# A transformer kernel on one core: the load, turning and rounding of the input at its start are rearranged

## The chip, the cores and the metric

The kernel runs on one core of a Trainium2 chip. The metric is the device time of one execution in microseconds, the median of several runs. One core has five engines that run their own instruction lists: TensorE (PE: matmuls; its weight loads are listed as PEld), VectorE (DVE), ScalarE (ACT), GpSimd (POOL) and SyncE (SP), which here only issues DMAs. They wait for one another through semaphores, and each one works strictly in the order of its list.

## The reference

Two blocks of a transformer over 256 positions of width 1024: the first has two layers, and each begins with a gated feed-forward part. What the change touches is only the very beginning, the first feed-forward part of the first layer:

```python
def rms_norm(x, g):
    y = xf * lax.rsqrt(jnp.mean(xf * xf, axis=-1, keepdims=True) + EPS)
    return (y * g)

def swiglu(x, w_gate, w_up, w_down):
    return (jax.nn.silu(x @ w_gate) * (x @ w_up)) @ w_down

h = x
h = h + 0.5 * swiglu(rms_norm(h, ffn1_norm_g[0]), ffn1_w_gate[0], ffn1_w_up[0], ffn1_w_down[0])
hn = rms_norm(h, mix_norm_g[0])
# mixing, a second feed-forward part; then the second layer and the second block
```

## The kernel before

**Arithmetic.** Everything is float32. A product of float32 matrices is made of three products of rounded halves: x = x_hi + x_lo and w = w_hi + w_lo, where the high half is the value rounded to the type that TensorE multiplies in one pass (fp32r), and the low half is the rounded rest; w_lo by x_lo is left out. The activations are kept turned (channels in partitions, 256 positions along the free axis), in eight chunks c of 128 channels; `hT` is the residual stream, `x_hi` and `x_lo` (`xh`, `xl`) are its halves multiplied by the gain `gcol` of the norm. The factor of the norm per position is applied later, to the product.

**Slots.** All weights pass through 403 slots of 128x1024 float32 (512 KB), in an order written out by `weight_plan`. SP loads slot j into one of seven raw buffers (it waits until `lo` of slot j-7 is made). ACT rounds it (`whi`, L1295, signal `hi`), DVE subtracts (`wlo`, L1896, signal `lo`), and TensorE consumes it in order. The split of slot j (`split_to`) also waits until TensorE has used slot j-5. When ACT and DVE come to `use(slot)`, they split up to slot+4.

**The matmuls of a slot** (`part`, `block`, L504): eight blocks, each a matmul of w_hi by both halves of x (512 columns) and one of w_lo by x_hi (256 columns). The first block of a slot waits for `hi` before its first and for `lo` before its second matmul. Slots 0 to 3 are the first pair of the first feed-forward part: slot 0 is gate, chunks 0 to 3; slot 1 up, chunks 0 to 3; slot 2 gate, chunks 4 to 7; slot 3 up, chunks 4 to 7. In slots 0 and 2 each chunk also waits for its `x_hi` and `x_lo`. Before slot 3 stand the sums of squares for the norm (`norm_sums`, four matmuls of `ones`, which wait for the last `square_sums`, that is `acc(0,3)`). Slot 4 begins when DVE has added the two halves of slot 2's product (`sum` of gate 0; ACT copies one half first, L1342, DVE adds, L1970).

**The start.** SP issues the gain row, the two tiles of 128 positions of `x` (512 KB each), then slots 0 to 3, then seven more gain rows, then the slots from 4 on. TensorE turns the gain row (8 transposes, L688), then `x`: 16 transposes (L696) into banks 0 to 3, one bank for each pair p of chunks, with a signal `x{p}` after each. ACT copies pairs 1 and 3 to `hT`, DVE pairs 0 and 2. Then ACT makes x_hi from `hT` (L1372, two for each pair), and after pairs 0 and 1 the w_hi of slots 0 and 1; DVE makes x_lo (L1988) and w_lo likewise. Then ACT squares the four pairs (L1362, the fourth waits for the first sum) and DVE adds them up (L1982, three times, `acc`). Slots 2 to 4 are split after that, by `use(0)`. On GpSimd masks and constants are made until 16.7 us (`ident` first, `alib` from 3.35 to 14.4 us).

Of the kernel before, what the change touches and what calls it, by code (L numbers as in the profile page):

```python
# [328 lines left out]
def signals(nc, ctx):  # L329
# [28 lines left out]
    s.ld_x = [sig(f"ld_x{i}", ["all"], 16) for i in T2]  # L358
# [56 lines left out]
    s.h_act = sig("h_act", [1, 3])  # L415
# [38 lines left out]
    s.h = sig("h", [(0, 0), (0, 2)] + [(v, p) for v in range(1, 7) for p in P4])  # L454
# [43 lines left out]
def tensor_engine(nc, B, s):  # L498
# [185 lines left out]
    def start():  # L684
        pe.wait_ge(*s.consts.at("ident"))
        pe.wait_ge(*s.ld_g0.at("all"))
        for c in range(8):
            t = pe.transpose(bank[4][:, c:c + 1], B.grow[0:1, c * 128:(c + 1) * 128], ident[0:1, 0:1])  # L688
        t.then_inc(*s.pe_set.now("g0"))
        for p in range(4):  # L690
            for tt in range(2):
                if p == 0:
                    pe.wait_ge(*s.ld_x[tt].at("all"))
                for j in range(2):
                    c = 2 * p + j
                    t = pe.transpose(bank[p][:, j * 256 + tt * 128:j * 256 + (tt + 1) * 128],  # L696
                                     B.xn[:, tt, c * 128:(c + 1) * 128], ident[:])
            t.then_inc(*s.pe_set.now(f"x{p}"))


    def ffn(f, x, gen):
        base, F = FFN[f], B.ffn[f]
        for p in range(PAIRS):
# [10 lines left out]
            if p:  # L714
                cols(x, 8, up_slot(f, p), 0)
                pe.wait_ge(*s.sum.at(("up", f, p - 1)))
                cols(x, 8, up_slot(f, p) + 2, 2)
            else:
                part(x, base, 0, range(4), True, False, gen)
                if f in (1, 3):  # L720
                    pe.wait_ge(*s.h.at((2, 2) if f == 1 else (5, 1)))
                elif f == 2:
                    pe.wait_ge(*s.sum.at(("up", 1, PAIRS - 1)))
                part(x, base + 1, 2, range(4), True, False)
                part(x, base + 2, 0, range(4, 8), False, True, gen)
# [554 lines left out]
def scalar_engine(nc, B, A, s):  # L1280
# [1558 lines left out]
def sync_engine(nc, B, A, s):  # L2839
# [99 lines left out]
```

## Time and profile before

| | us |
|---|---|
| median of 3 runs | 1253.1 |
| the runs | 1253.06, 1253.10, 1255.51 |
| the profiled execution, its own time | 1250.83 |
| its span in the trace | 1249.6 |
| TensorE busy | 1220.2 |

The span is the stretch of the trace from the first to the last instruction; 1.2 us of the execution's own time lie around it. A timeline row gives the start, the duration and the instruction; several of a kind in succession are merged into one row with their count (x14). In brackets is how long the engine stood idle before it and who released it. "L504" is the line of the helper in which all the products are written, so the names of the tiles tell which product it is: out<-in.

### The profile page before, as it was taken

The numbers are of one execution on the slowest core, as the hardware profiler recorded it, in microseconds if no ns is written. First come the engines' busy times: TensorE is split into PE (matmuls) and PEld (weight loads), VectorE is DVE, ScalarE is ACT, GpSimd is POOL, SyncE is SP. The second block draws the span as 40 slices with busy tenths as digits, with TensorE's granted clock in tenths as the row PEclk, the third lists the DMA queues.
The fourth block names the chain that finished last, engine by engine and source line by source line (L and its number), as shares of the span: only waits on it lengthen the run. The fifth ranks groups of instructions, "written<-read, shape, count | busy, mean of one in ns | idle before, by whom it ended". The sixth has DMA issues, their size and how long they took to land.

```text
span 1249.6 us, 18894 instructions
## 1 busy us (share of the span) xinstructions
PE 1220.2 (98%) x7518; PEld 1069.8 (86%) x7518; DVE 881.7 (71%) x1255; ACT 682.0 (55%) x1033; POOL 60.7 (5%) x89
## 2 busy tenths in 40 slices
PE   7999999989999999999999999999999999899998
PEld 6888888867888888888888887988888899788996
DVE  6686856885787766777766667587776668565875
ACT  5655544533665555555654457556655445555463
POOL 4000100100010000000000122000000000000000
PEclk9999999999999999999999999999999999999999
DMA  8766566771566655666655555156665665646450
GB/s 273 233 206 188 165 189 192 205 183 42 164 195 184 195 172 177 194 192 189 192 183 163 176 190 165 35 152 197 191 194 177 184 188 169 174 118 156 144 174 34
DMA packets 205653, 215.46 MB, mean 172 GB/s; under 512 B 9808, under 2 KB 192592, under 8 KB 205566
## 3 DMA queue, kind: packets, MB, share of 16 engines
q1 hardware_dynamic: 202998, 210.76, 56.8%
q10 hardware_dynamic: 2568, 3.50, 0.9%
q8 instruction: 60, 0.98, 0.3%
q14 instruction: 27, 0.22, 0.0%
HBM read 212.19 MB, written 2.03 MB: 171 GB/s over the span
## 4 chain that ended last, share of the span: by engine, by line
PE 92%; ACT 3%; DVE 2%; issue 1%; DMA 0%; ACTq 0%; POOL 0%; SPq 0%
PE psum L504 90%; ACT whi L1295 1%; DVE wlo L1896 1%; PE psum L668 0%; DMA xn<-in_x 0%; PE psum L953 0%; ACT qn L1599 0%; PE psum L696 0%; ACT L1735 0%; ACTq L1410 0%; DVE small L2333 0%; DVE oa L2543 0%; PE psum L1108 0%; ACT qkc L1699 0%; PE psum L906 0%
## 5 line engine op out<-in xcount | busy, mean ns | idle before, releaser
L504 PE MATMUL psum<-x,whi 128*128 128x512 f32 (+1 forms) x2288 | 696.2, 365 | 5.3 <-ACT whi L1295 2.4
L1896 DVE TENSOR_TENSOR wlo<-raw,whi 128x1024 fp32r<-128x1024 f32 (+2 forms) x403 | 474.3, 1189 | 193.3 <-ACT whi L1295 190.0
L504 PE MATMUL psum<-x,wlo 128*128 128x256 f32 x1960 | 549.3, 280 | 0.8 <-DVE wlo L1896 0.8
L1295 ACT CAST whi<-raw 128x1024 fp32r<-128x1024 f32 (+2 forms) x403 | 406.2, 1022 | 171.6 <-PE psum L504 162.5
L504 PEld LDWEIGHTS psum<-x,whi 128*128 128x128 f32 x2288 | 409.4, 189 | 79.6 <-ACT whi L1295 2.8
L504 PEld LDWEIGHTS psum<-x,wlo 128*128 128x128 f32 x1960 | 371.3, 189 | 1.5 <-DVE wlo L1896 1.3
L504 PE MATMUL psum<-g,whi 128*128 128x512 f32 x704 | 247.7, 396 | 0.0
L504 PE MATMUL psum<-g,wlo 128*128 128x256 f32 x704 | 197.6, 281 | 0.0
L504 PEld LDWEIGHTS psum<-g,whi 128*128 128x128 f32 x704 | 132.3, 188 | 31.8
L504 PE MATMUL psum<-whi,x 128*128 128x512 f32 (+1 forms) x512 | 141.2, 376 | 4.7 <-ACT va L1768 3.3
L504 PEld LDWEIGHTS psum<-g,wlo 128*128 128x128 f32 x704 | 132.2, 188 | 0.0
L504 PEld LDWEIGHTS psum<-whi,x 128*128 128x128 f32 x512 | 90.2, 190 | 21.1 <-ACT va L1768 3.5
L504 PE MATMUL psum<-wlo,x 128*128 128x512 f32 (+1 forms) x256 | 86.6, 374 | 0.0
L1342 ACT COPY pr<-psum 128x512 f32<-128x512 f32 x44 | 25.8, 586 | 66.9 <-PE psum L504 66.9
L1342 ACT COPY gr<-psum 128x512 f32<-128x512 f32 x44 | 25.8, 586 | 61.1 <-PE psum L504 61.1
L1970 DVE TENSOR_TENSOR pr<-psum,pr 128x512 f32<-128x512 f32 x44 | 30.4, 690 | 35.5 <-ACT pr L1342 35.5
L504 PEld LDWEIGHTS psum<-wlo,x 128*128 128x128 f32 x256 | 46.1, 189 | 8.6
L1372 ACT ACTIVATE x<-hT,gcol 128x256 fp32r<-128x256 f32 x64 | 28.5, 500 | 45.3 <-DVE hT L2105 28.8
L1970 DVE TENSOR_TENSOR gr<-psum,gr 128x512 f32<-128x512 f32 x44 | 30.4, 690 | 31.1 <-ACT gr L1342 31.0
L1988 DVE SCALAR_TENSOR_TENSOR x<-hT,gcol,x 128x256 fp32r<-128x256 f32 x64 | 28.7, 495 | 18.2 <-ACT x L1372 18.2
L1431 ACT ACTIVATE gr<-gr 128x512 f32<-128x512 f32 x44 | 27.6, 632 | 21.4 <-DVE gr L2054 21.3
L1440 ACT CAST g<-pr 128x512 fp32r<-128x512 f32 x44 | 27.4, 622 | 19.3 <-DVE pr L2062 19.3
(321 smaller groups left out, 851.1 us busy)
## 6 DMA issues: line engine op xcount, KB each, us to landing
raw<-in_ffn_w_gate SPq DMA_DIRECT2D x88, 512.0 KB, 4.5
raw<-in_ffn_w_up SPq DMA_DIRECT2D x88, 512.0 KB, 4.2
raw<-in_ffn_w_down SPq DMA_DIRECT2D x80, 512.0 KB, 3.8
raw<-in_w_in SPq DMA_DIRECT2D x52, 512.0 KB, 3.8
raw<-in_w_o SPq DMA_DIRECT2D x16, 512.0 KB, 4.7
raw<-in_a_w_in SPq DMA_DIRECT2D x14, 512.0 KB, 4.7
raw<-in_w_kv SPq DMA_DIRECT2D x16, 384.0 KB, 3.3
raw<-in_w_mem_kv SPq DMA_DIRECT2D x8, 512.0 KB, 3.7
```

What stands on the lines that cost most here:

```text
L504: return pe.matmul(o, l, r, start=start, stop=stop, skip_group_check=True)
L1295: act.copy(held(B.whi[:, i % SPLIT, :], *n), held(B.raw[:, i % RAW, :], *n)).then_inc(*s.hi.now(i))
L1342: act.copy(out, psum[:, b:b + 2, S:2 * S]).then_inc(*s.half.now(key))
L1372: act.activation(x[:, c, :], hT[:, c, :], ACT.Copy, scale=gcol[:, c, gi:gi + 1]).then_inc(*s.x_hi.now((gen, c)))
L1431: act.activation(r, r, ACT.Silu).then_inc(*s.silu.now((f, p)))
L1440: act.copy(F.gh[:, 2 * p:2 * p + 2, :], in_pairs(F.pr[:, p % 2, :])).then_inc(*s.g_hi.now((f, p)))
L1896: dve.tensor_tensor(held(B.wlo[:, i % SPLIT, :], *n), held(B.raw[:, i % RAW, :], *n), held(B.whi[:, i % SPLIT, :], *n).bitcast(F32), ALU.s ...
L1970: dve.tensor_tensor(out, psum[:, b:b + 2, 0:S], out, ALU.add).then_inc(*s.sum.now(key))
L1988: dve.scalar_tensor_tensor(out=xl[x][:, c, :], in0=hT[:, c, :], scalar=gcol[:, c, gi:gi + 1], in1=xh[x][:, c, :].bitcast(F32), op0=ALU.mul ...
```

## The change

- **Load.** The left 512 columns of `x` are loaded first (two DMAs of 256 KB), then slots 0 and 1, then the right 512 columns, then slots 2 and 3 and the rest as before. The first gain row is issued by ACT instead of SP.
- **TensorE.** After the gain row it does ten float32 matmuls of `ident` by `ident` (128x128, results not used), turns chunks 0 to 3 of `x` into banks 4 and 5, does six more such matmuls, and begins slot 0. The other eight transposes, into banks 6 and 7, stand in the middle of slot 1, after its fourth block.
- **ACT** makes x_hi straight from PSUM as each pair is turned, and splits one slot after each pair: slots 0 to 3. It copies no `hT`. Each of its squares waits for its pair of `hT`.
- **DVE** makes x_lo straight from PSUM and w_lo of the same slot, pair by pair; after pairs 1 and 3 it copies two pairs of `hT` (four copies in all, two before). The sums of squares stand behind all of this.

```diff
@@ TensorE, start
+            t = pe.transpose(bank[3][:, c:c + 1], B.grow[0:1, c * 128:(c + 1) * 128], ident[0:1, 0:1])
         t.then_inc(*s.pe_set.now("g0"))
+        warm(10)
+        x_turn("left", (0, 1))
+        warm(6)
+
+    def warm(n):
+        for _ in range(n):
+            mm(bank[2][:, 0:128], ident[:], ident[:], True, True)
+
+    def x_turn(side, pairs):
+        for tt in range(2):
+            pe.wait_ge(*s.ld_x[side, tt].at("all"))
+            for p in pairs:
                 for j in range(2):
                     c = 2 * p + j
-                    t = pe.transpose(bank[p][:, j * 256 + tt * 128:j * 256 + (tt + 1) * 128],
+                    t = pe.transpose(bank[4 + p][:, j * 256 + tt * 128:j * 256 + (tt + 1) * 128],
                                      B.xn[:, tt, c * 128:(c + 1) * 128], ident[:])
-            t.then_inc(*s.pe_set.now(f"x{p}"))
+                if tt == 1:
+                    t.then_inc(*s.pe_set.now(f"x{p}"))
@@ TensorE, ffn, slot 1
-                part(x, base + 1, 2, range(4), True, False)
+                part(x, base + 1, 2, range(4), True, False, None, (lambda: x_turn("right", (2, 3))) if f == 0 else None)
@@ ScalarE, squares and start
         if p == 0:
+            act.wait_ge(*s.h.at((v, 0)))
...
+            if v == 0:
+                act.wait_ge(*s.h.at((v, p)))
...
-        for p in (1, 3):
-            act.wait_ge(*s.pe_set.at(f"x{p}"))
-            act.copy(flat(hT[:, 2 * p:2 * p + 2, :]), bank[p]).then_inc(*s.h_act.now(p))
+        act.dma_start(B.grow[0:1, :], A["ffn1_norm_g"][0:1]).then_inc(*s.ld_g0.now("all"))
         act.wait_ge(*s.gcol.at("g0"))
         for p in range(4):
-            if p % 2 == 0:
-                act.wait_ge(*s.h.at((0, p)))
-            elif p == 1:
-                act.wait_ge(*s.h_act.at(3))
-            prep(0, p, [("f0", 0, xh[0])])
-            if p < 2:
-                split_to(p)
+            act.wait_ge(*s.pe_set.at(f"x{p}"))
+            for c in (2 * p, 2 * p + 1):
+                act.activation(xh[0][:, c, :], bank[4 + p][:, (c % 2) * S:(c % 2 + 1) * S], ACT.Copy,
+                               scale=gcol[:, c, 0:1]).then_inc(*s.x_hi.now(("f0", c)))
+            split_to(p)
@@ VectorE, start
-        for p in (0, 2):
-            dve.wait_ge(*s.pe_set.at(f"x{p}"))
-            dve.tensor_copy(flat(hT[:, 2 * p:2 * p + 2, :]), bank[p]).then_inc(*s.h.now((0, p)))
         for p in range(4):
-            prep(0, p, [("f0", 0, 0)])
-            if p < 2:
-                split_to(p)
+            dve.wait_ge(*s.x_hi.at(("f0", 2 * p + 1)))
+            for c in (2 * p, 2 * p + 1):
+                dve.scalar_tensor_tensor(out=xl[0][:, c, :], in0=bank[4 + p][:, (c % 2) * S:(c % 2 + 1) * S],
+                                         scalar=gcol[:, c, 0:1], in1=xh[0][:, c, :].bitcast(F32), op0=ALU.mult,
+                                         op1=ALU.subtract).then_inc(*s.x_lo.now(("f0", c)))
+            split_to(p)
+            if p % 2:
+                for q in (p - 1, p):
+                    dve.tensor_copy(flat(hT[:, 2 * q:2 * q + 2, :]), bank[4 + q]).then_inc(*s.h.now((0, q)))
@@ SyncE
-    sp.dma_start(B.grow[0:1, :], gains[0]).then_inc(*s.ld_g0.now("all"))
-    for tt in range(2):
-        sp.dma_start(B.xn[:, tt, :], A["x"][0, tt * 128:(tt + 1) * 128, :]).then_inc(*s.ld_x[tt].now("all"))
+    def x_load(side, c0):
+        for tt in range(2):
+            sp.dma_start(B.xn[:, tt, c0:c0 + 512], A["x"][0, tt * 128:(tt + 1) * 128, c0:c0 + 512]).then_inc(
+                *s.ld_x[side, tt].now("all"))
+
+    x_load("left", 0)
     for j, (w, k0, nk, c0, n) in enumerate(weight_plan(A)):
+        if j == 2:
+            x_load("right", 512)
```

## Rows read from the trace of the kernel before

**Rows 1.** The page: the chain that ended last, share of the span by engine.

```profile
PE 92%; ACT 3%; DVE 2%; issue 1%; DMA 0%; ACTq 0%; POOL 0%; SPq 0%
```

**Rows 2.** Waits of PE, whole span (columns: us in total, times, longest).

```profile
PE psum L504 <- issue: 5.9, 3, 4.4
PE psum L504 <- ACT va L1768: 3.3, 1, 3.3
PE psum L504 <- ACT whi L1295: 2.4, 1, 2.4
PE psum L696 <- DMA xn<-in_x: 2.3, 2, 1.6
```

**Rows 3.** Timeline of 0 to 10 us: start, duration, instruction, idle time before it.

```profile
0.79 0.34 SPq L2865 DMA_DIRECT2D gnm<-in_ffn_norm_g  x1
...
1.18 0.84 SPq L2867 DMA_DIRECT2D xn<-in_x  x2
...
2.28 0.98 PE L688 MATMUL psum<-ident,gnm 1*128 1x1 f32 x8 [2.28 <-DMA gnm<-in_ffn_norm_g]
...
4.90 0.69 PE L696 MATMUL psum<-ident,xn 128*128 128x128 f32 x2 [1.64 <-DMA xn<-in_x]
...
6.29 3.25 PE L696 MATMUL psum<-ident,xn 128*128 128x128 f32 x14 [0.71 <-DMA xn<-in_x]
...
7.02 0.69 DVE L2033 COPY hT<-psum 128x512 f32<-128x512 f32 x1 [3.55 <-PE psum L696]
```

**Rows 4.** Timeline of 10 to 14 us, all engines.

```profile
10.06 0.91 ACT L1372 ACTIVATE x<-hT,gcol 128x256 fp32r<-128x256 f32 x2
...
10.87 1.03 ACT L1295 CAST whi<-raw 128x1024 fp32r<-128x1024 f32 x1
...
11.94 1.55 DVE L1896 TENSOR_TENSOR wlo<-raw,whi 128x1024 fp32r<-128x1024 f32 x1 [0.45 <-ACT whi L1295]
...
12.56 1.86 POOL L2750 TENSOR_SCALAR_AFFINE_SELECT alib<-alib 128x1024 bf16<-128x1024 bf16 x1
...
13.41 1.70 DVE L1988 SCALAR_TENSOR_TENSOR x<-hT,gcol,x 128x256 fp32r<-128x256 f32 x2
...
13.54 0.58 PE L504 MATMUL psum<-x,wlo 128*128 128x256 f32 x1 [0.79 <-DVE wlo L1896]
```

**Rows 5.** Timeline of PE around 18 us: two block starts.

```profile
17.76 0.63 PE L504 MATMUL psum<-x,whi 128*128 128x512 f32 x1
...
18.39 0.40 PE L504 MATMUL psum<-x,whi 128*128 128x512 f32 x1
```

**Rows 6.** Timeline of DVE and ACT, 16 to 26 us.

```profile
16.19 1.66 DVE L1988 SCALAR_TENSOR_TENSOR x<-hT,gcol,x 128x256 fp32r<-128x256 f32 x4
17.78 2.27 DVE L1982 TENSOR_TENSOR acc<-acc,sqb 128x512 f32<-128x512 f32 x3
20.09 5.77 DVE L1896 TENSOR_TENSOR wlo<-raw,whi 128x1024 fp32r<-128x1024 f32 x5
...
19.03 4.84 ACT L1295 CAST whi<-raw 128x1024 fp32r<-128x1024 f32 x5
```

**Rows 7.** Timeline of PE at the square sums and the starts of slots 3, 4.

```profile
24.07 0.95 PE L504 MATMUL psum<-ones,acc 128*128 128x4 f32 x8
24.88 0.48 PE L504 MATMUL psum<-x,whi 128*128 128x512 f32 x1
...
27.74 0.39 PE L504 MATMUL psum<-x,whi 128*128 128x512 f32 x1
```

**Rows 8.** Timeline of PE: the norm rows of slot 5.

```profile
30.52 0.60 PE L504 MATMUL psum<-diag,ones 128*128 128x128 f32 x4
```

**Rows 9.** Windows after PE's longest gap; PEclk stands after the busy times.

```profile
272.00:274.00 2.00, 2.00 (x24) 1.34 (x20) 1.28 (x3) 0.00 (x0) 0.00 (x0) 0.50 1.10 348
274.00:276.00 2.00, 2.00 (x36) 1.14 (x27) 0.00 (x0) 0.00 (x0) 0.00 (x0) 0.91 0.54 182
```

**Rows 10.** DMA issues of 2.0 to 2.4 us: size each, us to landing.

```profile
raw<-in_ffn_w_gate SPq DMA_DIRECT2D x1, 512.0 KB, 5.7
```

More of the change, by code:

```diff
@@ L357, in signals @@
     s.ld_g0 = sig("ld_g0", ["all"], 16)
-    s.ld_x = [sig(f"ld_x{i}", ["all"], 16) for i in T2]
+    s.ld_x = {(d, i): sig(f"ld_x_{d}{i}", ["all"], 16) for d in ("left", "right") for i in T2}
     s.ld_gr = sig("ld_gains", range(1, 8), 16)
@@ L414, in signals @@
     s.row = sig("norm_row", NORM_ROWS)
-    s.h_act = sig("h_act", [1, 3])
     s.sq = sig("squares", h_pairs)
@@ L453, in signals @@
     s.gcol = sig("gain_cols", ["g0", "all"])
-    s.h = sig("h", [(0, 0), (0, 2)] + [(v, p) for v in range(1, 7) for p in P4])
+    s.h = sig("h", h_pairs)
     s.acc = sig("square_sums", [(v, p) for v in range(7) for p in range(1, 4)])
@@ L687, in start @@
         for c in range(8):
-            t = pe.transpose(bank[4][:, c:c + 1], B.grow[0:1, c * 128:(c + 1) * 128], ident[0:1, 0:1])
+            t = pe.transpose(bank[3][:, c:c + 1], B.grow[0:1, c * 128:(c + 1) * 128], ident[0:1, 0:1])
         t.then_inc(*s.pe_set.now("g0"))
-        for p in range(4):
-            for tt in range(2):
-                if p == 0:
-                    pe.wait_ge(*s.ld_x[tt].at("all"))
+        warm(10)
[8 more added lines that the diff above has]
+            for p in pairs:
                 for j in range(2):
                     c = 2 * p + j
-                    t = pe.transpose(bank[p][:, j * 256 + tt * 128:j * 256 + (tt + 1) * 128],
+                    t = pe.transpose(bank[4 + p][:, j * 256 + tt * 128:j * 256 + (tt + 1) * 128],
                                      B.xn[:, tt, c * 128:(c + 1) * 128], ident[:])
-            t.then_inc(*s.pe_set.now(f"x{p}"))
+                if tt == 1:
+                    t.then_inc(*s.pe_set.now(f"x{p}"))
     def ffn(f, x, gen):
@@ L2029, in start @@
         dve.wait_ge(*s.pe_set.at("g0"))
-        dve.tensor_copy(gcol[:, :, 0], bank[4][:, 0:8]).then_inc(*s.gcol.now("g0"))
-        for p in (0, 2):
-            dve.wait_ge(*s.pe_set.at(f"x{p}"))
-            dve.tensor_copy(flat(hT[:, 2 * p:2 * p + 2, :]), bank[p]).then_inc(*s.h.now((0, p)))
+        dve.tensor_copy(gcol[:, :, 0], bank[3][:, 0:8]).then_inc(*s.gcol.now("g0"))
         for p in range(4):
-            prep(0, p, [("f0", 0, 0)])
-            if p < 2:
-                split_to(p)
+            dve.wait_ge(*s.x_hi.at(("f0", 2 * p + 1)))
[7 more added lines that the diff above has]
+                    dve.tensor_copy(flat(hT[:, 2 * q:2 * q + 2, :]), bank[4 + q]).then_inc(*s.h.now((0, q)))
         for p in range(4):
@@ L2864, in sync_engine @@
              A["ffn2_norm_g"][1:2], A["norm_pre_2"][0:1]]
-    sp.dma_start(B.grow[0:1, :], gains[0]).then_inc(*s.ld_g0.now("all"))
-    for tt in range(2):
-        sp.dma_start(B.xn[:, tt, :], A["x"][0, tt * 128:(tt + 1) * 128, :]).then_inc(*s.ld_x[tt].now("all"))
+    def x_load(side, c0):
[3 more added lines that the diff above has]
+    x_load("left", 0)
     for j, (w, k0, nk, c0, n) in enumerate(weight_plan(A)):
+        if j == 2:
+            x_load("right", 512)
         if j == 4:
```

1 line of the change is left out of this document (removed).

## The prediction

> **What bounds the kernel now.** I read the chain that ended last first: 92% of it is TensorE, next to nothing is DMA [rows 1]. Then the list of what TensorE waited for [rows 2]. Its waits are few, each behind another engine that works on a product of TensorE's own. Only at the start does it wait for data. From slot 4 on nothing is tied to the clock on the wall, so whatever the start wins or loses should reach the end one to one. I therefore follow the start to one mark, the first matmul of slot 4, at 27.74 us [rows 7], and compare times there.
>
> The path to that mark now: the input lands, TensorE turns it from 4.90 to 9.54 us [rows 3]; ACT rounds x from 10.06 and slot 0 from 10.87, DVE makes its rest from 11.94 to 13.49, and at 13.54 TensorE goes on [rows 4]. From there it never stops. A block starts 0.63 us after the one before it at 17.76 [rows 5], but a whole slot of eight takes 27.74 - 24.88 = 2.86 us later, 0.357 a block [rows 7]: TensorE ran at 1.2 GHz until about 18.2 us and at 2.4 GHz after it. The granted clock shows the lower level only where it fell within the span: 0.50 in 272 to 274 us and 0.91 in 274 to 276 [rows 9], after the wait of 4.4 us; the wait of 3.3 us is not followed by such a stretch [rows 2]. DVE has done the last sum of squares at 20.05 [rows 6], and TensorE asks for it at 24.07 [rows 7]: 4 us to spare.
>
> **Load and constants.** The gain row stays first on its queue, now ACT's, with nothing ahead of it; I take the same arrival and the same end of its transposes, 3.26 us [rows 3]. If ACT's queue were slower, all shifts by that. SP comes to x 0.4 us sooner, with half the bytes ahead of slot 0, which now lands at about 2.1 + 5.7 = 7.8 us [rows 10]; the left half is there by 4.9 at the latest. Neither is late for what follows, because ten matmuls of constants stand ahead of the transposes. The trace has no such matmul by name, but its like: the norm rows are two float32 matmuls in the code and four records in the trace [rows 8], the sums of squares four and eight [rows 7]. So ten constants are twenty passes. One pass at 1.2 GHz I take from the transposes of the same shape: 14 in 3.25 and 2 in 0.69 [rows 3] make 2.56 / 12 = 0.213 us. At 2.4 GHz it is half, 0.107. Bounds: 10 x 0.107 = 1.1 us (one pass each, full clock) and 20 x 0.232 = 4.6. I take 20 x 0.213 = 4.3, end at 7.55.
>
> When does the clock rise? In this trace TensorE had worked for 4.65 us from 13.54, and from 270.64 (after the long wait) until about 274.4, 3.7 us. Counted from the gain row or from the first constant that is 5.9 to 7.9; I take 7.5. Then six transposes at 0.107 and the 0.27 until the last is through put pair 0 at 8.4. The price of the bounds: a rise at 5.9 saves 1.6 / 0.213 x 0.107 = 0.8 us, one at 9.2 or later costs six transposes at 0.107, 0.65, and some blocks, in all 1.0.
> The Trainium skill (TensorE: Matmul & The Clock Gate, What's actually happening) says that the number of slow matmuls at the start varies between runs of one kernel, and not to fit a model to one count; by that the 7.5 is not a property of the kernel, and the sum would be anything between the two bounds. The single trace here cannot show that spread.
>
> **To slot 0.** Pair 0 is there at 8.4; ACT needs 0.91 for x_hi and 1.03 for the rounding [rows 4], 10.4; DVE 1.23 for w_lo (five in 5.77 are 1.15 each and a tail, [rows 6]): 11.7 against 13.49. Gain 1.8 us: the copy to `hT` is off this path. The six later constants take 0.64 to 1.3 us and lie in TensorE's wait for ACT: nothing. x_hi straight from PSUM is not in the trace; a DVE operation of 512 columns from PSUM takes 0.69 [rows 3], about two rests of 256 (0.83, [rows 6]), so I take the same cost, with 0.1 us either way for each of four steps on the path, 0.4.
> DVE was slow while GpSimd ran its select on `alib` (12.56 to 14.42): 1.55 for a w_lo that takes 1.23 elsewhere, 1.70 for two x_lo where four take 1.66 [rows 4, 6]. Two x_lo of pair 1 will again fall at 11.7; at the slow rate w_lo of slot 1 comes at 14.9, 0.4 late.
> The Trainium skill (GPSIMD Engine Reference, Key points) says that GpSimd and VectorE contend where a VectorE instruction has two inputs in SBUF; an x_lo from PSUM has one, so by the rule it would keep its 0.42 us each and the 0.4 would be gone. I leave them out of the sum and in the range.
>
> **Slot 0.** If the clock has risen before it, 0.357 a block: from the arrival of w_lo 2.86 - 0.24 = 2.6 us instead of 18.39 - 13.54 = 4.85 [rows 4, 5]. Gain 2.25; end at 14.3. TensorE then idles at most some 1.3 us ahead of it, and even 3.3 us cost no clock [rows 2].
>
> **Slot 1** now holds eight transposes: 8 x 0.107 = 0.87 lost (they stood ahead of everything before). End at 14.3 + 2.86 + 0.87 = 18.0.
>
> **Slot 2 is where a new wait comes.** ACT and DVE can do nothing for it until pair 2 is turned: 14.3 + 4 x 0.357 + 5 x 0.107 + 0.27 = 16.55. Then x_hi 0.91 and the rounding of slot 2, 1.03, queued behind it: 18.5; w_lo 1.23: 19.8. TensorE would have been through slot 2 at 20.9; it now gets there at 19.8 + 2.6 = 22.4. Loss 1.5.
>
> **Slot 3 is where the second comes,** the sums of squares. DVE's list after w_lo of slot 2: two x_lo 0.83, w_lo of slot 3 1.15, two copies of `hT` 1.3 (0.69 each, overlapping), then the three sums with ACT's square between them, which took 20.09 - 17.78 = 2.3 [rows 6]. That is 19.8 + 5.6 = 25.4; TensorE asks at 22.4. Loss 3.0; the 4 us to spare are gone, because `hT` of the right half is copied only behind slot 3's split. Sums and slot 3 take 0.81 + 2.86 [rows 7], end at 29.05.
>
> **Slot 4.** Slots 4 to 6, which DVE split at 20 to 26 us beside TensorE [rows 6], now queue behind the sums: from 25.7 (ACT rounds slot 4 after its last square) 3 x 1.15, to 29.2, then the sum of gate 0, 0.69: 29.85. Loss 0.8. Mark: 29.85 against 27.74.
>
> **Sum.** -1.8 - 2.25 + 0.87 + 1.5 + 3.0 + 0.8 = 2.1 us later. The profiled execution, 1250.8, would be 1252.9. It lies 2.3 below the median of the runs shown; the shift is added to the median: 1253.1 + 2.1 = 1255.2. Own range of this case: 0.8 + 0.4 down and 1.0 + 0.4 + 0.4 up, 1254.0 to 1257.0. What a measurement of this kernel can tell from no change is about 0.2%, 2.5 us, so most of this case counts as the same.
>
> **Rivals.**
> - **The clock stays low (slower).** The change doesn't do what it says: matmuls of constants, or what the later gaps leave of them, don't lift the clock, as 3.25 us of transposes up to 9.54 did not [rows 3]. It decides if the rise comes after slot 0. Then pair 0 is ready at 9.1, 0.7 later, and slots 0 and 1 run some 9 to 14 blocks at 0.63 instead of 0.357, 2.5 to 3.8 us: 2.1 + 0.7 + 3.2 = 6.0 less some of the waits behind, about 5.3: 1258.4. For it: the same rows; against it: the stretch now is 6 us long and unbroken.
> - **The constants are short.** One pass each, 2.1 us, end at 5.4, pair 0 at about 6.9 with the clock up in the meantime: 1.5 less, +0.6, 1253.7. Against it: the doubled records [rows 7, 8].
> - **The waits at slots 2 to 4 don't come (faster).** If ACT and DVE had slack for the right half, by much cheaper operations from PSUM, 5.3 us of loss would vanish and 3.2 of gain stay: 1249.9. It takes halving DVE's 5.6 us behind slot 2 and more, and its nearest rows (0.69 from PSUM, 1.15, 2.3) give nothing of the kind. Halfway there the result is the same as before.
>
> **How the numbers follow.** The forecast gets 0.62, the low clock 0.12, short constants 0.16, no waits 0.10. Slower by over 2.5 us: the low clock, and of the forecast, with an error of a run's median of a microsecond, 0.36 of it: 0.12 + 0.22 = 0.34. Faster: 0.10 and little of the short constants: 0.12. Same: 0.54. The range leaves out the last rival and the upper half of the low clock: 1251.3 to 1258.3.
>
> **What would show it.** Twenty records of constants from 3.3 to about 7.6 us; pair 0 turned at 8.4; blocks 0.36 apart from the first of slot 0; TensorE idle for about 1 us before the second matmul of slot 2, about 3 us before the matmuls of `ones` and `acc`, under 1 us before slot 4, the releasers w_lo, the last `acc` and the gate sum on DVE; from there on the same waits as before. The prediction is wrong if a block of slot 0 takes 0.63, if the sums of squares come before TensorE asks, or if the gain row comes later on ACT's queue.

## The result, and the profile after

| | before | after |
|---|---|---|
| median, us | 1253.1 | 1259.5 |
| the runs, us | 1250.4 to 1255.5 | 1258.0 to 1260.3 |
| the profiled execution, us | 1250.8 | 1259.8 |
| its span, us | 1249.6 | 1258.6 |
| first product of slot 4, us | 27.74 | 32.57 |

The ratio of after to before is 1.0044, with a 95% interval of 1.0032 to 1.0057: 4.0 to 7.1 us slower, 5.5 in the middle. Forecast were 2.1 slower and a range that ended at 1258.3. The direction is right, the size forecast was under half of what came.

The chain that ended last is TensorE's as before (page of after, shares of the span; it answers to [rows 1]), so the difference lies in what TensorE waited for:

```profile
PE 91%; ACT 3%; DVE 3%; issue 1%; ACTq 0%; DMA 0%; POOL 0%
```

Waits of TensorE in after (us in total, times, longest), which answer to [rows 2]. The first is new; those for w_lo and w_hi are now two each:

```profile
PE psum L503 <- DVE acc L1990: 2.5, 1, 2.5
PE psum L503 <- DVE wlo L1904: 2.4, 2, 1.7
...
PE psum L503 <- ACT whi L1305: 1.9, 2, 1.6
```

Timeline of after, 0 to 14 us, all engines (the product's helper is L503 here); it answers to [rows 3, 4]:

```profile
3.18 4.29 PE L503 MATMUL psum<-ident 128*128 128x128 f32 x20
...
7.30 1.04 PE L705 MATMUL psum<-ident,xn 128*128 128x128 f32 x8
...
8.18 1.50 PE L503 MATMUL psum<-ident 128*128 128x128 f32 x12
8.21 1.28 ACT L1409 ACT_TABLE_LOAD   x1 [8.21 <-PE psum L705]
...
11.29 1.07 POOL L2759 TENSOR_SCALAR_AFFINE_SELECT alib<-alib 128x1024 bf16<-128x1024 bf16 x1
11.31 2.13 DVE L1904 TENSOR_TENSOR wlo<-raw,whi 128x1024 fp32r<-128x1024 f32 x1
...
11.33 0.50 PE L503 MATMUL psum<-x,whi 128*128 128x512 f32 x1 [1.65 <-ACT whi L1305]
...
12.50 1.85 POOL L2761 TENSOR_SCALAR_AFFINE_SELECT alib<-alib 128x1024 bf16<-128x1024 bf16 x1
13.36 0.86 DVE L2042 SCALAR_TENSOR_TENSOR x<-psum,gcol,x 128x256 fp32r<-128x256 f32 x2
...
13.49 0.39 PE L503 MATMUL psum<-x,wlo 128*128 128x256 f32 x1 [1.66 <-DVE wlo L1904]
```

These two rows stand in the timeline of the kernel before, 0 to 14 us:

```profile
0.79 1.28 ACT L1394 ACT_TABLE_LOAD   x1 [0.79 <-PEq L2929]
...
11.32 1.09 POOL L2748 TENSOR_SCALAR_AFFINE_SELECT alib<-alib 128x1024 bf16<-128x1024 bf16 x1
```

The ten constants are twenty records and end when they should. But at 8.21 us, when pair 0 is there, ACT first loads its activation table for 1.28 us; before, the same load stood at 0.79 us and cost nothing. And DVE's first w_lo takes 2.13 us beside GpSimd's selects, so TensorE goes on at 13.49, where it had gone on at 13.54.

That the two times are so near is no accident. In both kernels w_lo ends 1.08 us after the end of GpSimd's first select (12.36 and 13.44 in after, 12.41 and 13.49 before), though it began at 11.31 in one and at 11.94 in the other. So w_hi, ready 0.6 us earlier in after, gained nothing: DVE got no further until the select was over.

Then the clock. Windows of after (busy us of PE, PEld, DVE, ACT, POOL, then PEclk, DMA share, GB/s):

```profile
14.00:16.00 2.00, 2.00 (x8) 1.64 (x7) 2.00 (x4) 0.00 (x0) 1.57 (x4) 0.50 1.09 346
16.00:18.00 2.00, 2.00 (x10) 1.73 (x9) 0.63 (x2) 0.00 (x0) 0.42 (x2) 0.70 1.09 348
```

TensorE had worked without a pause until 9.7 us and was at 2.4 GHz (twelve passes in 1.50 us, 8.18 to 9.68). It then waited 1.65 us, did one matmul, waited 1.66 us, and from about 13.9 to 17.2 us the granted clock was 0.50. Slot 0 ran at 0.64 us a block again.

The second half of the start, which answers to [rows 6, 7]:

```profile
21.80 0.49 PE L503 MATMUL psum<-x,whi 128*128 128x512 f32 x1 [0.25 <-ACT whi L1305]
...
23.06 0.39 PE L503 MATMUL psum<-x,wlo 128*128 128x256 f32 x1 [0.77 <-DVE wlo L1904]
...
26.04 2.28 DVE L1990 TENSOR_TENSOR acc<-acc,sqb 128x512 f32<-128x512 f32 x3
...
28.41 3.50 DVE L1904 TENSOR_TENSOR wlo<-raw,whi 128x1024 fp32r<-128x1024 f32 x3
...
28.47 1.03 PE L503 MATMUL psum<-ones,acc 128*128 128x4 f32 x8 [2.55 <-DVE acc L1990]
...
32.57 0.50 PE L503 MATMUL psum<-x,whi 128*128 128x512 f32 x1 [0.19 <-DVE gr L1978]
```

Here is what the prediction's steps for slots 2 to 4 describe: the short waits of slot 2, 2.55 us for the last `acc`, then DVE's three splits and the gate sum. At slot 4 after is 4.83 us behind. By 51.93 (46.36 before) it is 5.57, 0.6 of the growth being one DMA issue on ACT's queue that took 1.04 us instead of 0.45. Up to 815 us nothing is added. That 5.57 is what the ratio gives (5.5; the two medians are 6.4 apart). The rest of the 9.0 between the two spans comes at late waits, and the run of the kernel before shows below that such losses come without the change too.

### The profile page after: what moved, and what is told of

The parts are those of the page before. It is cut to its first block, busy times and chain, and to the rows that moved or that the text cites. A ratio compares the mean times of both kernels' runs of the same rounds, so it can differ in the third digit from the quotient of the medians.

```text
span 1258.6 us, 18961 instructions
## 1 busy us (share of the span) xinstructions
PE 1227.1 (97%) x7550; PEld 1077.1 (86%) x7550; DVE 883.0 (70%) x1257; ACT 680.6 (54%) x1031; POOL 60.4 (5%) x89
## 4 chain that ended last, share of the span: by engine, by line
PE 91%; ACT 3%; DVE 3%; issue 1%; ACTq 0%; DMA 0%; POOL 0%
PE psum L503 90%; DVE wlo L1904 1%; ACT whi L1305 1%; PE psum L667 0%; PE psum L963 0%; ACT qn L1607 0%; ACT qT L1668 0%; ACTq L1418 0%; ACT L1743 0%; DVE small L2344 0%; DVE oa L2554 0%; PE psum L1118 0%; ACT qkc L1707 0%; PE psum L916 0%; PE psum L1255 0%
## 5 line engine op out<-in xcount | busy, mean ns | idle before, releaser
L503 PE MATMUL psum<-x,whi 128*128 128x512 f32 (+1 forms) x2288 | 696.8, 366 | 5.6 <-ACT zob L1716 2.0
L503 PE MATMUL psum<-x,wlo 128*128 128x256 f32 x1960 | 550.4, 281 | 2.4 <-DVE wlo L1904 2.4
L503 PEld LDWEIGHTS psum<-x,whi 128*128 128x128 f32 x2288 | 410.4, 190 | 79.2 <-ACT zob L1716 2.4
L503 PEld LDWEIGHTS psum<-x,wlo 128*128 128x128 f32 x1960 | 372.3, 190 | 3.1 <-DVE wlo L1904 3.1
L503 PE MATMUL psum<-g,whi 128*128 128x512 f32 x704 | 247.7, 396 | 0.0
L503 PE MATMUL psum<-g,wlo 128*128 128x256 f32 x704 | 197.9, 281 | 0.0
L503 PEld LDWEIGHTS psum<-g,whi 128*128 128x128 f32 x704 | 132.4, 188 | 31.7
L503 PE MATMUL psum<-whi,x 128*128 128x512 f32 (+1 forms) x512 | 143.0, 380 | 4.7 <-ACT va L1776 3.3
L503 PEld LDWEIGHTS psum<-g,wlo 128*128 128x128 f32 x704 | 132.2, 188 | 0.0
L503 PEld LDWEIGHTS psum<-whi,x 128*128 128x128 f32 x512 | 91.3, 192 | 21.2 <-ACT va L1776 3.5
L503 PE MATMUL psum<-wlo,x 128*128 128x512 f32 (+1 forms) x256 | 87.4, 377 | 0.0
L503 PEld LDWEIGHTS psum<-wlo,x 128*128 128x128 f32 x256 | 46.7, 191 | 8.9
L1384 ACT ACTIVATE x<-hT,gcol 128x256 fp32r<-128x256 f32 x56 | 25.0, 500 | 45.3 <-DVE hT L2116 28.8
L1996 DVE SCALAR_TENSOR_TENSOR x<-hT,gcol,x 128x256 fp32r<-128x256 f32 x56 | 24.4, 484 | 17.0 <-ACT x L1384 17.0
```

What stands on the lines that cost most here:

```text
L503: return pe.matmul(o, l, r, start=start, stop=stop, skip_group_check=True)
L1384: act.activation(x[:, c, :], hT[:, c, :], ACT.Copy, scale=gcol[:, c, gi:gi + 1]).then_inc(*s.x_hi.now((gen, c)))
L1996: dve.scalar_tensor_tensor(out=xl[x][:, c, :], in0=hT[:, c, :], scalar=gcol[:, c, gi:gi + 1], in1=xh[x][:, c, :].bitcast(F32), op0=ALU.mul ...
```

## The experiments

The first product of slot 4 is the mark, as in the prediction (27.74 before, 32.57 after). Medians are read with the ratio to runs of the kernel before on the same chip. Every mark is from one trace, and the two don't go together one to one: e7_onlyconst has its mark 1.5 us later and the same median as the kernel before, e12_wholerows_noconst 3.9 earlier and a median that is, by the ratio, only 0.8 to 3.4 lower.

**e4_before: the kernel before again.** No edit.

> The kernel before once more, to see its own spread and how its granted clock goes with its time. In the changed kernel's trace 3.4 of the 9.0 us come at two late waits of TensorE (3.3 us at 1093, 2.0 us at 1145), after which its matmuls ran at 1.2 GHz; in the trace of before they didn't. If that is chance from run to run, some executions of before have it too: spans from 1249 to 1254 us, the longer ones with a lower mean clock (0.992 or less against 0.996). If it belongs to the change: all executions within 1 us of one another and a clock of 0.996.

Measured: ratio 0.999 (0.9981 to 0.9999), 1250.9 to 1255.3 us, mark at 27.70. The same window at TensorE's late wait of 3.3 us, first in the first trace of the kernel before, then in this one:

```profile
1090.00:1095.00 5.00, 3.26 (x16) 2.69 (x17) 1.97 (x4) 3.30 (x8) 0.00 (x0) 1.00 0.10 40
```

```profile
1090.00:1095.00 5.00, 2.38 (x6) 1.92 (x7) 1.51 (x4) 4.16 (x9) 0.00 (x0) 0.75 0.26 95
1095.00:1100.00 5.00, 5.00 (x25) 4.17 (x24) 1.61 (x5) 1.75 (x6) 0.00 (x0) 0.91 0.37 105
```

In the same program the clock falls after this wait in one execution and not in another. In after's trace it fell there for longer (18 matmuls in 6.31 us, which took 3.69 before):

```profile
1096.84 6.31 PE psum L503 x18
```

Over 96 executions of the kernel before (all those that the experiments ran), the eight with a mean granted clock of 0.996 took 1250.8 us on average, the 36 with 0.994 took 1253.5, the eleven with 0.990 took 1255.5. So the kernel's spread of 5 us goes largely with its clock, and the late falls in after's trace need be no work of the change. Whether the change makes them more frequent was not tried. The chance half of the expectation holds; the 0.992 and 0.994 groups, hardly apart (1253.7 and 1253.5), say that the mean clock is not all of it.

**e1_table: the table load moved out of the path.**

```diff
         act.dma_start(B.grow[0:1, :], A["ffn1_norm_g"][0:1]).then_inc(*s.ld_g0.now("all"))
+        act.wait_ge(*s.consts.at("ones"))
+        act.activation(small[0:1, 319:320], B.ones[0:1, 0:1], ACT.Copy)
         act.wait_ge(*s.gcol.at("g0"))
```

> One element is copied by ACT right after the gain row's DMA, so that the activation table is loaded at about 2 us and not at 8.21 us behind the wait for pair 0. My theory, that the table load stands on the path and pushes w_lo of slot 0 into GpSimd's select: x_hi from about 8.25 us, w_lo of slot 0 takes about 1.3 us instead of 2.13 and ends at about 11.3 (13.4 in the changed kernel), slot 0 runs at 2.4 GHz, 0.36 us a block from its first, and the first matmul of slot 4 comes 3.0 to 3.8 us earlier than in the changed kernel (32.57). Median about 1256. Rival, that GpSimd's work alone slows w_lo: the start is 1.3 us earlier, but w_lo still takes about 2 us and the clock still falls: 1.3 us or less, about 1258.

Measured: ratio 1.0018 (1.0001 to 1.0035), median 1256.6; w_lo of slot 0 takes 1.23 us and ends at 11.0; slot 0 at 0.35 us a block; the mark is 29.42. ACT, then DVE:

```profile
1.33 1.28 ACT L1406 ACT_TABLE_LOAD   x1 [1.33 <-PEq L2948]
```

```profile
9.77 1.23 DVE L1906 TENSOR_TENSOR wlo<-raw,whi 128x1024 fp32r<-128x1024 f32 x1
```

Slot 3 begins 3.96 us earlier than in after (25.39 against 29.35). But then the clock fell in this trace, after the 2.59 us wait for `acc` (timeline row, then the window):

```profile
24.50 1.03 PE L503 MATMUL psum<-ones,acc 128*128 128x4 f32 x8 [2.59 <-DVE acc L1992]
```

```profile
28.00:30.00 2.00, 2.00 (x8) 1.71 (x7) 1.05 (x4) 0.34 (x1) 0.73 (x1) 0.50 1.06 360
```

What follows: the table load cost more than its 1.28 us, since it also pushed w_lo into GpSimd's select and stretched TensorE's wait. The waits behind slot 1 are untouched by it. Here w_lo of slot 1 (11.70 to 12.92) was under way before the select, and this time the select waited:

```profile
11.85 1.99 POOL L2761 TENSOR_SCALAR_AFFINE_SELECT alib<-alib 128x1024 bf16<-128x1024 bf16 x1
```

It took 1.99 us for its 1.07. The two engines seem to take turns by whole instructions; that is read from these rows and was not tried by itself.

**e6_poollater: GpSimd's selects after w_lo of slot 1.** Built on after.

```diff
+        pool.wait_ge(*s.lo.at(1))
         step(pool.affine_select(out=B.alib[:, 0], in_=B.alib[:, 0], compare_op=ALU.is_ge, ...
```

> Built on the changed kernel: GpSimd starts its two selects on alib only after DVE has made w_lo of slot 1. If the selects made w_lo of slot 0 slow: 1.23 us instead of 2.13, it ends at 12.55 instead of 13.45 and the mark comes 0.9 us earlier; the idle stretch of TensorE shrinks from 1.66 to 0.8 us before it, and if the clock then stays up, another 1.6: median 1257 to 1258.6. If something else made it slow (the DMA writes into the raw buffers, say): 2.1 us again and no change.

Measured: ratio 1.0034 (1.0021 to 1.0048), median 1257.7, 1257.5 to 1258.7. w_lo takes 1.23 us and no block of slot 0 is slow, though pair 0 was there only at 9.5, because the eight transposes still ran at 1.2 GHz (1.74 us, 1.04 in after):

```profile
12.61 1.23 DVE L1904 TENSOR_TENSOR wlo<-raw,whi 128x1024 fp32r<-128x1024 f32 x1
```

TensorE waited 1.61 and 0.76 us around its first matmul, and the clock stayed up. The mark is 31.38, 1.2 earlier than in after. It was the selects that slowed w_lo; the loads went on as before.

**e3_bridge: more constants.** The second group is 14 instead of 6.

```diff
-        warm(6)
+        warm(14)
```

> The second group of constants is 14 instead of 6, so TensorE works until about 11.2 us instead of 9.7. If the clock fell at about 13.9 because TensorE had been idle or nearly so since 9.7, it now stays up: slot 0 at 0.36 us a block, its end 1.6 us earlier, slot 4 1.6 us earlier, since the chain of DVE starts from the middle of slot 1: median about 1257.9. Rival, that this length doesn't matter, as it is the wait for w_lo that counts: the clock falls as before and nothing changes, 1259.5.

Measured: ratio 1.0035 (1.0018 to 1.0053), median 1257.8, 1254.0 to 1261.9. The constants now reach up to the first product, and the blocks after the wait are 0.35 apart:

```profile
8.62 3.29 PE L503 MATMUL psum<-ident 128*128 128x128 f32 x28
...
13.50 0.39 PE L503 MATMUL psum<-x,wlo 128*128 128x256 f32 x1 [1.23 <-DVE wlo L1904]
13.72 0.40 PE L503 MATMUL psum<-x,whi 128*128 128x512 f32 x1
...
14.07 0.40 PE L503 MATMUL psum<-x,whi 128*128 128x512 f32 x1
```

The clock stayed up through slot 0, as the theory wanted; in this trace it fell after the wait for `acc` instead (blocks 0.64 apart from 28.85 on), and the mark is 32.22, 0.35 before that of after. One fall was traded for another. The median moved by what was expected, but with a spread of 8 us that is no proof.

**e2_noconst: no constants at all.** Both `warm` calls are taken out of after.

> Both groups of constants (ten and six) are left out. If the constants cost more than they bring, because the clock falls again before slot 0 anyway: pair 0 is turned at about 5.5 us instead of 8.1, the table load and the roundings follow, w_lo of slot 0 ends at about 10.2, all of slot 0 and some of slot 1 run at 1.2 GHz (2.9 us lost for the ten blocks instead of 1.6), and slot 4 begins 1.5 to 2.5 us earlier than in the changed kernel: median about 1257.5. Rival, that the constants earn their place: the whole start at 1.2 GHz costs more than 3 us, median 1260 or more.

Measured: ratio 1.0026 (1.0016 to 1.0036), median 1257.6. The transposes begin at 3.67 and w_lo of slot 0 is there at 9.7, at 1.2 GHz:

```profile
3.67 1.97 PE L703 MATMUL psum<-ident,xn 128*128 128x128 f32 x8
...
9.68 0.58 PE L503 MATMUL psum<-x,wlo 128*128 128x256 f32 x1 [0.47 <-DVE wlo L1902]
```

Slot 0 ran at 0.64 us a block until 13.3, and the mark is 29.77, 2.8 us earlier than in after. The first ten constants held the transposes back by 3.6 us, more than the clock gave back; the theory that they cost more than they bring holds. 0.9 of the gain comes by way of GpSimd: w_lo was over (9.63) before the first select began, and took 1.23 us instead of 2.13.

**e5_asklater: the sums of squares are asked for one slot later.** Built on e1_table; the norm rows behind them move by one slot too.

```diff
-NORM = ((3, 5), (75, 4), (101, 4), (169, 4), (237, 0), (269, 6), (337, 4))
+NORM = ((4, 5), (75, 4), (101, 4), (169, 4), (237, 0), (269, 6), (337, 4))
```

> Built on e1_table: the sums of squares are asked for before slot 4 instead of before slot 3 (and the norm rows before slot 6). In e1_table TensorE waits 2.6 us there, from 21.9 to 24.5, and its clock falls afterwards. If that wait is the loss: slot 3 runs at once, slot 4 begins 2 us or more earlier than in e1_table, median about 1254. If DVE's total work is the bound, as I think: TensorE now waits before slot 4 for the gate sum, which DVE ends at about 28.5 us as before, and the sums come on top, 0.9; slot 4's first product at about 29.4, 0.7 later than in e1_table. What is won is only the clock, up to 1.5 us in those executions in which it falls: 1256 to 1257.

Measured: ratio 1.0037 (1.0022 to 1.0052), median 1258.6, so no faster than e1_table (the two intervals overlap). Slot 3 begins at once, at 22.0, and TensorE then waits 3.83 us for the gate sum:

```profile
28.82 1.87 PE L503 MATMUL psum<-ones,acc 128*128 128x4 f32 x8 [3.83 <-DVE gr L1980]
```

DVE ends that sum at 28.77, in e1_table at 28.55. So the wait for `acc` is not the loss; it is where DVE's backlog shows first. Taken away there, it comes back one slot later and longer. After it the clock fell again, and the first product of slot 4 came at 30.55, later than the 29.4 expected.

**e9_turnfirst: the right half turned ahead of slot 0.** Built on e1_table.

```diff
         x_turn("left", (0, 1))
         warm(6)
+        x_turn("right", (2, 3))
...
-                part(x, base + 1, 2, range(4), True, False, None, (lambda: x_turn("right", (2, 3))) if f == 0 else None)
+                part(x, base + 1, 2, range(4), True, False)
```

> Built on e1_table: the eight transposes of the right half stand after the second group of constants, ahead of slot 0, instead of in the middle of slot 1. Everything else, DVE's order with its late copies and sums too, stays. If the late turning is what makes the waits at slots 2 and 3: w_lo of slot 2 is made at about 16.5 us (19.1 in e1_table), no wait before slot 2, slot 2 ends at about 19.5, and the wait before slot 3 begins sooner but ends sooner too, at about 22 (24.5 in e1_table). Slot 4 at about 26 instead of 28.9 to 30: median about 1253.5. If DVE's work alone sets the end of slot 3's wait: it still ends at 24 or later, 1256.

Measured: ratio 1.0001 (0.999 to 1.0012), median 1254.4. Mark 26.49:

```profile
22.40 1.03 PE L503 MATMUL psum<-ones,acc 128*128 128x4 f32 x8 [2.18 <-DVE acc L1993]
...
26.49 0.50 PE L503 MATMUL psum<-x,whi 128*128 128x512 f32 x1 [0.18 <-DVE gr L1981]
```

DVE works from 9.52 to 26.4 with no gap of more than 0.1 us. In e1_table it stood idle for 2.77 us ahead of its x_lo at 16.89, until pair 2 had come through TensorE and ACT:

```profile
16.89 0.88 DVE L2044 SCALAR_TENSOR_TENSOR x<-psum,gcol,x 128x256 fp32r<-128x256 f32 x2 [2.77 <-ACT x L1411]
```

DVE's list begins 0.69 us later than in e1_table (9.52 against 8.83) and saves the 2.77 of that gap: 2.08 net, and its gate sum indeed ends at 26.44 instead of 28.55, 2.11 earlier. The rest of what the mark gained on the 29.42 of e1_table is that trace's fallen clock. So the late turning is the cause of the waits at slot 2, which are gone, and it put DVE's gate sum, and slot 4 with it, 2.1 us later. The wait for `acc` is hardly shorter (2.18 us, 2.59 in e1_table); it only lies earlier: there DVE's order, with its late copies and sums, is the likely cause, since e8_whole and e11_wholerows, whose order differs (and not it alone), have no such wait. With the late turning and the table load gone, the change costs nothing that the ratio shows, and with constants and all it gains nothing either.

**e7_onlyconst: constants alone in the kernel before.**

```diff
         t.then_inc(*s.pe_set.now("g0"))
+        warm(3)
         for p in range(4):
...
             t.then_inc(*s.pe_set.now(f"x{p}"))
+        warm(8)
```

> The kernel before with constants alone: three after the gain row and eight after the last transpose of x, both inside waits of TensorE (1.6 and 2.4 us). If constants raise the clock and cost nothing inside a wait: the transposes begin at 4.9 as before, slot 0's w_lo comes at 13.5 as before, and slot 0 runs at 0.36 us a block instead of 0.64: slot 1 starts 2.2 us earlier, the mark 2 us earlier if DVE keeps up (it has 4 us to spare at the sums, but slots 2 to 6 queue behind them), median 1251.5 to 1252. Rival: DVE has no such slack, its split of slot 2 (from 20.1 us) and of the slots behind is the next bound, then at most 1 us is won, 1253.

Measured: ratio 0.9998 (0.9988 to 1.0008), median 1253.5. Slot 0 and slot 1 ran at 0.35 us a block, as hoped, and ended at 18.9. Then slot 2 wasn't there, because ACT splits slots 2 to 6 only behind its squares. ACT, then TensorE:

```profile
18.98 4.82 ACT L1300 CAST whi<-raw 128x1024 fp32r<-128x1024 f32 x5
```

```profile
20.06 0.49 PE L504 MATMUL psum<-x,whi 128*128 128x512 f32 x1 [0.82 <-ACT whi L1300]
21.32 0.39 PE L504 MATMUL psum<-x,wlo 128*128 128x256 f32 x1 [0.76 <-DVE wlo L1901]
```

```profile
22.00:24.00 2.00, 2.00 (x8) 1.71 (x8) 2.00 (x3) 1.80 (x2) 0.00 (x0) 0.50 0.66 193
```

Waits of 0.82 and 0.76 us, and at about 22 us the clock fell; the mark is 29.20, 1.5 later than without constants. The rival holds: 2.2 us won in slots 0 and 1 were given back, in this trace and more; the ratio says neither gain nor loss.

**e10_halfloads: the kernel before with four loads of half rows.**

```diff
-    for tt in range(2):
-        sp.dma_start(B.xn[:, tt, :], A["x"][0, tt * 128:(tt + 1) * 128, :]).then_inc(*s.ld_x[tt].now("all"))
+    for side, c0 in (("left", 0), ("right", 512)):
+        for tt in range(2):
+            sp.dma_start(B.xn[:, tt, c0:c0 + 512], A["x"][0, tt * 128:(tt + 1) * 128, c0:c0 + 512]).then_inc(
+                *s.ld_x[tt].now(side))
```

> The kernel before with x loaded by four DMAs of 256 KB (both tiles' left halves, then both right halves) instead of two of 512 KB, and nothing else; the transposes wait for the halves of the right. In e8_whole such loads ran at 190 to 270 GB/s from 3 to 6 us, where the kernel before has 374 to 397, and slot 0 landed at 9.7 us instead of 7.8. If the size or the row length of the loads does that: x is complete at about 8.1 instead of 6.3, w_lo of slot 0 is made at about 15.3 instead of 13.5, and the median is 1.8 us up, 1255.3. If it was something else in e8_whole (the gain row on ACT's queue, TensorE's work): x complete at 6.3 and 1253.5.

Measured: ratio 1.0008 (0.9994 to 1.0021), median 1255.1. The same window in the kernel before and here (GB/s stands last):

```profile
3.00:6.00 3.00, 0.95 (x5) 0.46 (x4) 0.17 (x1) 0.00 (x0) 2.75 (x4) 1.00 1.00 387
```

```profile
3.00:6.00 3.00, 0.49 (x5) 0.40 (x4) 0.17 (x1) 0.00 (x0) 2.75 (x4) 1.00 0.69 196
```

```profile
7.81 3.80 PE L696 MATMUL psum<-ident,xn 128*128 128x128 f32 x16 [4.32 <-DMA xn<-in_x]
...
15.51 0.58 PE L504 MATMUL psum<-x,wlo 128*128 128x256 f32 x1 [0.98 <-DVE wlo L1896]
```

x is complete at 7.8 instead of 6.3 and w_lo of slot 0 at 15.5 instead of 13.5: the traces show the loads' cost plainly, the medians only lean the same way. Part of it may be SP's own: it took 1.77 us to issue the four loads and 0.84 for the two, so that the last piece of x was asked for about 0.9 us later. The mark, 30.18, is 2.4 later.

**e8_whole: everything of x ahead of slot 0.** Built on e1_table: both halves loaded and turned first, two constants between them and four after; new orders on ACT and DVE.

```diff
+        hi(0)          # ScalarE: hi(p) = x_hi of pair p from PSUM
+        hi(1)
+        split_to(0)
+        hi(2)
+        split_to(1)
+        hi(3)
+        squares(0, 0)
+        squares(0, 1)
+        split_to(2)
...
+        lo(0)          # VectorE: lo(p) = x_lo from PSUM, rows(q) = the copy to hT
+        lo(1)
+        rows(0)
+        split_to(0)
+        lo(2)
+        split_to(1)
```

> Built on e1_table: both halves of x are loaded ahead of slot 0 and turned ahead of it (two constants between them, four after), still rounded straight from PSUM, nothing in the middle of slot 1; ACT and DVE round two pairs of x, slot 0, a pair, slot 1, a pair, and the sums of squares stand behind slot 2's split. If the right half's late turning is what costs: w_lo of slot 0 at about 9.7 us, no wait before slot 3, under 1.5 us before slot 4, which begins at 23 to 25 us, 3 to 4.5 before the kernel before (27.74): median 1249 to 1251, faster than before. If ACT and DVE are the bound whatever the order, because their work up to slot 6 is the same and starts no earlier than at 8: slot 4 no earlier than 27 us, median 1253.

Measured: ratio 0.9992 (0.9981 to 1.0004), median 1251.7. No wait for `acc`, 1.01 us for the gate sum, mark 25.27, 2.5 before the kernel before; but slot 0's weights landed only at 9.66, behind the half loads:

```profile
9.66 1.04 ACT L1306 CAST whi<-raw 128x1024 fp32r<-128x1024 f32 x1 [2.54 <-DMA raw<-in_ffn_w_gate]
```

```profile
25.27 0.51 PE L503 MATMUL psum<-x,whi 128*128 128x512 f32 x1 [1.01 <-DVE gr L1991]
```

**e11_wholerows: whole rows.** Built on e8_whole: two loads of 512 KB, transposes tile by tile, three constants before and four after; ACT copies pairs 1 and 3 to `hT`, each ahead of its x_hi, DVE pairs 0 and 2.

```diff
-    x_load("left", 0)
-    x_load("right", 512)
+    for tt in range(2):
+        sp.dma_start(B.xn[:, tt, :], A["x"][0, tt * 128:(tt + 1) * 128, :]).then_inc(*s.ld_x[tt].now("all"))
...
         hi(0)
-        hi(1)
         split_to(0)
-        hi(2)
+        rows(1)
+        hi(1)
         split_to(1)
+        hi(2)
+        rows(3)
         hi(3)
```

> Built on e8_whole: x loaded by two DMAs of whole rows, turned tile by tile ahead of slot 0 (three constants before, four after); ACT rounds each pair straight from PSUM and slots 0 and 1 between them, and copies pairs 1 and 3 to hT, DVE pairs 0 and 2; slots 2 and 3 are split around the sums. Expected: slot 0 landed at 7.8, w_lo of slot 0 at 10 to 11 (13.5 in the kernel before), slot 0 at 0.36 us a block, at most 1 us of wait before slot 4, which begins at 23.5 to 24.5, 3 to 4 us before the kernel before: median about 1250. If DVE's list up to slot 6 is the bound: slot 4 at 26 or later and the wait before it over 2 us, 1252.

Measured: ratio 0.9973 (0.9958 to 0.9988), median 1252.2, 1247.4 to 1254.1. ACT's first x_hi, then TensorE at slots 0 and 4:

```profile
6.87 0.84 ACT L1415 ACTIVATE x<-psum,gcol 128x256 fp32r<-128x256 f32 x2 [4.04 <-PE psum L706]
```

```profile
9.99 0.39 PE L504 MATMUL psum<-x,wlo 128*128 128x256 f32 x1 [0.79 <-DVE wlo L1926]
...
23.79 0.49 PE L504 MATMUL psum<-x,whi 128*128 128x512 f32 x1 [1.01 <-DVE gr L2000]
```

w_lo of slot 0 is there at 9.94 instead of 13.49, and the mark comes at 23.79, 3.95 before the kernel before. By the ratio it is 1.5 to 5.3 us faster than the kernel before, and so faster than both kernels.

**e12_wholerows_noconst: the same without constants.** The `warm` calls are out.

> e11_wholerows without any constants. If the clock at slot 0 is worth something here: slots 0 and 1 begin at 0.64 us a block for 3 to 5 us, slot 4 begins 1 to 2 us later than in e11_wholerows, 1251.5. If DVE's list sets slot 4 in any case, as it did with constants alone in the kernel before: under 0.5 us of difference.

Measured: ratio 0.9984 (0.9973 to 0.9994), median 1251.4; the mark is 23.84, the same to 0.05 us:

```profile
4.45 3.67 PE L704 MATMUL psum<-ident,xn 128*128 128x128 f32 x16 [1.16 <-DMA xn<-in_x]
...
8.78 0.50 PE L504 MATMUL psum<-x,whi 128*128 128x512 f32 x1 [0.65 <-ACT whi L1304]
...
10.26 0.40 PE L504 MATMUL psum<-x,whi 128*128 128x512 f32 x1
```

Slot 0 already ran at 2.4 GHz, with the sixteen transposes (at 1.2 GHz) ahead of it and a wait of only 0.65 us between. The constants do nothing here that the traces can show; the two intervals overlap, and both lie below 1.

## Why the prediction was wrong

**What held.** The gain row came at 2.27 us on ACT's queue; the ten constants were twenty passes and ended at 7.47 (7.55 forecast); pair 0 was turned at 8.2 (8.4). Rounding straight from PSUM cost what the like from SBUF cost: two x_hi 0.84, two x_lo 0.88. The transposes in slot 1 took 0.8. The new wait of slot 2 cost 1.5 us (1.5 forecast), the wait for `acc` 2.7 (3.0), slot 4 0.4 (0.8). Their causes are those that the prediction named. ACT and DVE can't begin on pair 2 until it is turned in the middle of slot 1: with that gone, e9_turnfirst has no wait at slot 2. And the copies and sums stand late in DVE's list: e9_turnfirst keeps 2.18 us of the wait for `acc`. e5_asklater shows that DVE's backlog is the bound.

The losses came as forecast, then; what failed was the gain ahead of them. Of the 1.8 us forecast up to w_lo of slot 0 next to nothing came (13.44 against 13.49), and of the 2.25 in slot 0 came 0.6.

**What failed, step "To slot 0": 1.75 us.** The sum had w_lo at 11.7, it came at 13.44. First, ACT's table load, 1.28 us. The prediction counted "the copy to `hT` is off this path" as a gain and did not ask what else stood with the first activation. In the kernel before the load ran at 0.79 us, while ACT waited for its first pair; after the edit it ran behind that wait. Neither the diff nor the trace of before says so, but the load had a row of its own on the page's timeline, and it should have been asked what places it there. e1_table puts the price at 1.28 us and more. Second, GpSimd's select: 0.9 us. The prediction had it only from the second select on and for the x_lo of pair 1; the slot's own w_lo was taken at 1.23 because it was to be over by 11.7. Moved later by the table load, it began 0.02 us behind the first select and took 2.13. The 1.55 of [rows 4] lay beside the selects nearly as fully; it is shorter only because that w_lo began later, with the first select half over. The same holds in three more traces: begun at 11.70, 11.76 and 11.84 (e4_before, e3_bridge, e7_onlyconst), w_lo ended at 13.44 or 13.45. e6_poollater confirms the price. Against these 2.2 us, pair 0 came 0.2 earlier than forecast and ACT's two steps took 0.2 less, which leaves about 1.75.

The Trainium skill (GPSIMD Engine Reference, Key points) says that VectorE instructions with two inputs in SBUF contend with GpSimd. The traces agree where the select was first: w_lo, with two such inputs, took 2.13 us beside it and 1.23 without it, and two x_lo read from PSUM took 0.86 beside it at 13.36, where from SBUF they had taken 1.70. Where w_lo was first (e1_table, slot 1), it kept its 1.22 and the select paid. The prediction left this out of the sum and looked for it in the wrong instruction.

**What failed, step "Slot 0": 1.64 us.** "TensorE then idles at most some 1.3 us ahead of it, and even 3.3 us cost no clock." It idled 1.65 and 1.66 us with one matmul between, and the clock fell; blocks of slot 0 at 0.63 us were the prediction's own sign of being wrong. The row used, a wait of 3.3 us without a fall, was one draw: e4_before has a fall after the same wait, and e7_onlyconst one behind waits of 0.82 and 0.76 us. e1_table, e3_bridge and e6_poollater, which each shorten the idle stretch, kept the clock up through slot 0; that fits, but each is one trace of a thing that varies. So the fall and its price are shown, and why it came in this trace stays open.

1.75 and 1.64, less 0.7 from the waits at slots 3 and 4, which came out shorter, make the 2.7 by which the mark missed (4.83 against 2.11). The remaining 0.7 up to 52 us is mostly the one long DMA issue; whether the change has a part in it was not tried.

**The rivals.** "The clock stays low" came near in its total (5.3 us, 5.5 measured), but by luck: the constants did lift the clock (twelve passes in 1.50 us), it was lost again before it was used, and the slow blocks cost 1.64 us where the rival had 2.5 to 3.8 and a late pair 0. Most of the rest is the table load and the select, which it did not have. The constants were not short, and the waits did come. The range ended too low, because it took the clock's fall as all or nothing and had no term for an instruction that no line of the kernel asks for.

**Where the intended gain went.** In after, the clock that the constants bought was gone at 13.9 us. In e7_onlyconst, where it held through slots 0 and 1, ACT's late splits gave it back. In e12_wholerows_noconst no constants were needed. What does pay is the rest of the change in another order: 3.95 us at the mark in e11_wholerows. That run rounds straight from PSUM, turns all of x first, loads the table ahead and splits slots 2 and 3 earlier; what each of these brings was not tried apart.

## What to carry to other kernels

Draw the list of every engine up to the first point where the new order meets the old one, and sum the work of the slower helpers: here a gap of 2.8 us on DVE became waits on TensorE three slots on, and moving the question only moved the wait. When the first activation of a kernel moves behind a wait, look at where its table load goes, and put a one-element activation ahead if need be. Filling a wait with constants is worth something only if the work behind it is ready when TensorE is, and if there is no second wait before it. Where DVE and GpSimd both work from SBUF, look at which of them starts first: here 0.6 us won on ACT were lost because DVE still came second.

## What was not expected of the hardware

- Four loads of 256 KB with rows of 2 KB moved 196 GB/s in 3 to 6 us, two of 512 KB with rows of 4 KB 387, although the weights' loads of 512 KB have rows of only 1 KB and move 347 to 382 (e10_halfloads against the kernel before). Whether the size of a load, its rows or the time to issue it does it was not tried.
- The granted clock falls after a given wait in some executions and not in others of one program (e4_before); in e7_onlyconst it fell behind waits of 0.82 and 0.76 us. The Trainium skill (TensorE: Matmul & The Clock Gate, What's actually happening) says of the start of a kernel that its slow stretch varies from run to run; here two traces of one program agree (up at 18.2 us before, at 17.2 in e4_before), and it holds at the later waits too, where it goes with most of the kernel's spread of 5 us.
- With sixteen transposes from 4.45 to 8.12 us and a wait of 0.65 us, the clock was up at the first matmul of slot 0, at 8.78 (0.50 us for 512 columns, e12_wholerows_noconst); in the kernel before, where the sixteen ended at 9.54 and a wait of 2.41 us followed, the same matmul took 0.79 at 11.95, and the clock was up only at 18.2 [rows 3 to 5]. The wait does not settle it: with the same 2.41 us in e10_halfloads that matmul took 0.50, and the clock was gone again at the next, at 15.51.
- Wherever a w_lo on DVE and a select on GpSimd met in these traces, the one that began first kept its length to about 0.1 us and the other took 0.3 to 0.9 us more.
